# Buffers of TensorE's operands at other addresses, the first weight panel on SyncE's queue, four weight splits at other places

## The chip, the cores and the metric

The program runs on one core of one Trainium2 chip. The metric is the device time of one execution in microseconds (us); a kernel's time is the median of several executions. TensorE (PE) multiplies, VectorE (DVE) and ScalarE (ACT) work on elements, GpSimd (POOL) builds a few tables, and SyncE (SP) issues most DMAs.

## What is computed

Three transformer layers over 256 tokens of width 1024, all in float32. Cut to what matters:

```python
def first_block(x, ...):
    h = x
    for layer in range(2):
        y = rmsnorm(h, norm_g[layer, 0])
        y = gmlp_mixer(y, ...) if layer == 0 else diff_attention(y, ...)
        h = h + rmsnorm(y, norm_g[layer, 1])
        y = rmsnorm(h, norm_g[layer, 2])
        y = conv_ffn(y, ...)                 # D_FF = 2816: (gelu(g) * u) @ w_down
        h = h + rmsnorm(y, norm_g[layer, 3])
    return h

def second_block(x, ...):                    # one layer
    x = x + 0.5 * swiglu(rms_norm(x, ffn1_norm), ...)
    u = rms_norm(x, mix_norm) @ w_in
    a_out = mla_attention(...)               # 8 heads, low-rank q and kv, rope
    b_out = moba_attention(...)              # 8 heads of 64, linear distance bias
    x = x + concatenate([a_out, b_out]) @ w_out
    x = x + 0.5 * swiglu(rms_norm(x, ffn2_norm), ...)
    return rms_norm(x, final_norm)
```

`reference` is `second_block(first_block(x))`. The weights fill 352 panels of 128 x 1024 numbers, 512 KB each, and each is used once.

## The kernel before, in words

**Stages.** The panels run in the order gMLP mixer (`GMLP`, 24), convolutional FFN (`FFN0`, 66), differential attention (`DIFF`, 32), FFN (`FFN1`), SwiGLU FFN (`FFN2`), the MLA and MoBA mixer (`MIX`, 32), SwiGLU FFN (`FFN3`). Between two stages stands a `boundary`: the residual is added, the row is normed and turned by TensorE, and the next stage's first four panels are taken.

**A panel's way.** SyncE's `load(n)` (L312 to L317) brings panel n into one of five `raw` buffers; from the sixth on it first waits until the low split of panel n-5 is done (semaphore `lo`). ScalarE's `upto(last)` (L441) casts each panel up to `last` into `w_high`, in float32r (L448); VectorE's `upto(last)` (L864) subtracts that from `raw` into `w_low` (L868). Both have nine buffers (`RING`). TensorE multiplies `high * x_high + high * x_low + low * x_high`, in float32r. Activations are split in the same way into `x_parts` (X2), `a_high`, `a_low`, `c4_high`, `c4_low`. In every float32r product one operand is a panel and the other an activation part. In the rows, `G<-x_parts,w_high` has `x_parts` moving and `w_high` stationary; `G<-w_high,x_parts` has it the other way round.

**An FFN.** Gate and up panels are multiplied with `wide_tile` (L1407 for the high part against both activation parts, 512 columns; L1411 for the low part, 256 columns). Down panels are multiplied in `rows` (L1487, 512 columns each). The last seven down panels stand at the end of each FFN (`_ffn_order`), and `tail` multiplies them token half by token half.

**Order.** Every engine runs a list that is written out by hand, and semaphores join the lists. Where a split stands in the list of ScalarE or VectorE is set by the calls of `upto` between other steps. A step behind a split waits for it, and a split behind a step waits for the step.

**The start.** TensorE runs itself up with products of `ones` (`run_up(12)`, then `run_up(4)` after the first activation part). ScalarE's queue issues the DMA of panel 0 (L635) and then that of `g0`, the first norm's gains (L636). SyncE issues the turned input `xT` in four parts (L331), panels 1, 2, 3, 4, the relative-position rows, panels 5 and 6, the input and the constants, panel 7, and so on. ScalarE then makes the high activation parts (`x0_high`, L643) and casts the panels; VectorE makes the low ones (`x0_low`, L1075). The first products are L1422 and L1426, the further ones of the first eight panels L1442, L1443 and L1448. Panels 0 to 3 are used for both token halves, then 4 to 7 for the first half, then 4 to 7 for the second.

**The second mixer.** Its heads 8 to 11 (two MoBA heads each) and 12 to 15 (two MLA heads each) run through: scores (L1598, L1599), `combine` (VectorE), `exps` (ScalarE, L614, L616), `turn` (TensorE, L1615), `turned_out` (ScalarE, L627), `weigh_values` (TensorE, L1627 to L1629), `outs` (VectorE, L1314), `pair_out` (TensorE, L1848), `cast` (ScalarE, L811), `low_out` (VectorE, L1322). `pair_out(15)`, the last, waits for `outs(15)` and for `low_out(14)`. `qk_out(10)` (L632, L633) makes what `scores(10)` reads. `B` in the code is `MIX`, so `upto(B + 35)` splits the last of the four panels with which `FFN3` begins. In `boundary(6)` TensorE needs panel B + 35 last of the four.

**Addresses.** The tensors lie one behind the other in the order of their `sb(...)` calls, each start rounded up to 32 bytes. `raw`, `w_high` and `w_low` start at multiples of 64 bytes. `h` follows with 2 x 1026 numbers, 8208 bytes, and so `x_parts`, `a_high`, `a_low`, `c4_high`, `c4_low`, the gains, `big1` and `big2` start 32 bytes beside a multiple of 64. `big2` has 8208 bytes too, after which `big3`, `w3`, `qk` and the tables are at multiples of 64 again. The identity for the turns lies in `cst`, 32 bytes beside.

## Time and profile before

| | us |
|---|---|
| median of 3 runs | 1078.57 |
| lowest, highest | 1077.62, 1079.41 |
| the profiled execution, its own time | 1076.99 |
| its span, first to last instruction | 1075.1 |

The profile is of one execution; the rows' times are counted from its first instruction. 1.9 us of the execution's time lie outside the span. Its granted TensorE clock was 0.999 on the mean. In a row of the timeline stand the start, the time until the last of the row's instructions ended, the engine, the line, the operation, and in brackets how long the engine had been idle and what ended that.

### The profile page before, as it was taken

What the parts mean: (1) busy time and instruction counts of PE and PEld (TensorE: products, weight loads), DVE (VectorE), ACT (ScalarE), POOL (GpSimd) and SP (SyncE); (2) the same over time, 40 slices, a digit from 0 to 9 for tenths busy, and PEclk for the clock granted to TensorE, in tenths of its full rate; (3) what the DMA queues carried; (4) which work ended last, traced back from release to release, by engine and by line L of the source; (5) the groups of instructions that cost most, each with busy time, mean ns of one, the idle gap of its engine ahead of it and who ended that gap; (6) DMA issues with size and microseconds to landing.
All of it is one profiled execution on the core that took longest, in us unless ns stands there. A gap on an engine that the chain in (4) does not pass through costs nothing.

```text
span 1075.1 us, 15630 instructions
## 1 busy us (share of the span) xinstructions
PE 1064.2 (99%) x5976; PEld 910.3 (85%) x5976; DVE 774.0 (72%) x1213; ACT 653.2 (61%) x1176; POOL 36.3 (3%) x39
## 2 busy tenths in 40 slices
PE   8999999999999999999999999999999999999997
PEld 7988888888799878888888888888899878888886
DVE  4898987878767889878787666656676857655663
ACT  5767755666657777666567554445456647444552
POOL 0840000000000000000000000000000000000000
PEclk9999999999999999999999999999999999999999
DMA  9764866655463357656553756665355516656641
GB/s 344 260 199 149 241 203 200 222 181 177 172 219 114 104 159 247 199 179 212 180 197 130 238 176 188 212 197 187 129 171 152 197 58 206 189 192 196 198 157 40
DMA packets 56777, 198.13 MB, mean 184 GB/s; under 512 B 6576, under 2 KB 8536, under 8 KB 56704
## 3 DMA queue, kind: packets, MB, share of 16 engines
q1 hardware_dynamic: 56016, 195.89, 56.3%
q10 hardware_dynamic: 576, 1.05, 0.3%
q8 instruction: 48, 0.79, 0.3%
q14 instruction: 25, 0.20, 0.1%
q0 software_dynamic: 112, 0.20, 0.1%
HBM read 195.35 MB, written 1.25 MB: 183 GB/s over the span
## 4 chain that ended last, share of the span: by engine, by line
PE 95%; ACT 2%; DVE 2%; DMA 1%; issue 0%; ACTq 0%
PE G L1407 28%; PE Y L1487 27%; PE G L1411 14%; PE G L1392 3%; PE G L1394 3%; PE G L1393 3%; PE G L1442 2%; PE G L1448 2%; PE G L1443 2%; PE Y L1482 2%; PE Y L1392 1%; PE Y L1393 1%; PE Y L1394 1%; PE G L1461 1%; PE G L1615 1%; PE Y L1495 1%
## 5 line engine op out<-in xcount | busy, mean ns | idle before, releaser
L868 DVE TENSOR_TENSOR w_low<-raw,w_high 128x1024 fp32r<-128x1024 f32 x352 | 424.5, 1224 | 38.0 <-ACT w_high L448 36.4
L448 ACT CAST w_high<-raw 128x1024 fp32r<-128x1024 f32 x352 | 363.1, 1045 | 13.8 <-DMA raw<-in_panels 8.9
L1407 PE MATMUL G<-x_parts,w_high 128*128 128x512 f32 x1280 | 325.3, 396 | 0.0
L1407 PEld LDWEIGHTS G<-x_parts,w_high 128*128 128x128 f32 x1280 | 233.1, 188 | 49.3
L537 ACT COPY big<-G 128x512 f32<-128x512 f32 x80 | 46.8, 585 | 233.0 <-PE G L1411 233.0
L1411 PEld LDWEIGHTS G<-x_parts,w_low 128*128 128x128 f32 x1280 | 172.7, 188 | 14.6
L1411 PE MATMUL G<-x_parts,w_low 128*128 128x256 f32 x1280 | 175.8, 280 | 0.0
L962 DVE TENSOR_TENSOR w<-G,big 128x512 f32<-128x512 f32 x80 | 55.3, 691 | 161.9 <-ACT big L537 161.8
L1487 PE MATMUL Y<-w_high,a_high 128*128 128x512 f32 x420 | 134.0, 400 | 0.0
L1487 PE MATMUL Y<-w_high,a_low 128*128 128x512 f32 x420 | 132.3, 396 | 0.0
L1487 PE MATMUL Y<-w_low,a_high 128*128 128x512 f32 x420 | 132.1, 395 | 0.0
L1487 PEld LDWEIGHTS Y<-w_high,a_low 128*128 128x128 f32 x420 | 79.0, 188 | 19.1
L1487 PEld LDWEIGHTS Y<-w_low,a_high 128*128 128x128 f32 x420 | 79.0, 188 | 19.1
L1487 PEld LDWEIGHTS Y<-w_high,a_high 128*128 128x128 f32 x420 | 73.0, 188 | 11.4
L989 DVE SCALAR_TENSOR_TENSOR w<-w,par 128x255 f32<-128x255 f32 (+1 forms) x160 | 70.2, 480 | 1.3
L1392 PE MATMUL G<-x_parts,w_high 128*128 128x256 f32 x224 | 63.7, 285 | 0.0
L1393 PE MATMUL G<-x_parts,w_high 128*128 128x256 f32 x224 | 62.6, 280 | 0.0
L1394 PE MATMUL G<-x_parts,w_low 128*128 128x256 f32 x224 | 62.6, 279 | 0.0
L1442 PE MATMUL G<-w_high,x_parts 128*128 128x512 f32 x120 | 48.7, 406 | 0.1
L565 ACT ACTIVATE w<-w,par 128x256 f32<-128x256 f32 x80 | 43.6, 594 | 8.4 <-DVE w L962 8.4
L1443 PE MATMUL G<-w_low,x_parts 128*128 128x512 f32 x120 | 47.5, 395 | 0.0
L1448 PE MATMUL G<-w_high,x_parts 128*128 128x512 f32 x120 | 47.5, 395 | 0.0
(256 smaller groups left out, 1204.8 us busy)
## 6 DMA issues: line engine op xcount, KB each, us to landing
raw<-in_panels SPq DMA_DIRECT2D x351, 512.0 KB, 4.3
gain_pre<-in_gains SPq DMA_DIRECT2D x7, 512.0 KB, 5.8
gain_post<-in_gains SPq DMA_DIRECT2D x4, 512.0 KB, 6.6
big<-in_xT SPq DMA_DIRECT2D x4, 256.0 KB, 7.1
h<-in_x SPq DMA_DIRECT2D x2, 512.0 KB, 7.2
big<-rel_rows SPq DMA_DIRECT2D x8, 128.0 KB, 5.2
raw<-in_panels ACTq DMA_DIRECT2D x1, 512.0 KB, 5.3
big<-in_w_s SPq DMA_DIRECT2D x1, 512.0 KB, 9.3
```

The source lines that it names most:

```text
L448: s.copy(WH[:, n % RING, :], raw[:, n % RAWS, :]).then_inc(hi, 1)
L868: v.tensor_tensor(WL[:, n % RING, :], raw[:, n % RAWS, :], WH[:, n % RING, :].bitcast(F32), ALU.subtract).then_inc(lo, 1)
L989: last = v.scalar_tensor_tensor(out=wb[:, f % 2, m, T - n:T], in0=gate_of(f, m)[:, 0:n], scalar=par[:, c:c + 1], in1=wb[:, f % 2, m, T - n ...
L1392: mm(out, WH[:, j, c:c + w], xh, start=first, stop=False, skip_group_check=skip)
L1393: mm(out, WH[:, j, c:c + w], xl, start=False, stop=False, skip_group_check=skip)
L1394: return mm(out, WL[:, j, c:c + w], xh, start=False, stop=last, skip_group_check=skip)
L1407: mm(out, WH[:, n % RING, k * P:(k + 1) * P], X2[:, k, :, :], start=k == 0, stop=False, skip_group_check=True)
L1411: last = mm(out[:, 0:T], WL[:, n % RING, k * P:(k + 1) * P], X2[:, k, 0, :], start=False, stop=k == KT - 1, skip_group_check=True)
L1442: mm(out, xh, hic, start=k == 0, stop=False)
L1443: mm(out, xh, loc, start=False, stop=False)
L1448: last = mm(out, xl, hic, start=False, stop=k == KT - 1)
L1487: end = mm(Y[:, 2 * t + c, :], x, w[:, j, half(c)], start=start, stop=stop)
```

## The change

1. `x_parts`, `a_high`, `a_low`, `c4_high` and `c4_low` are allocated straight behind `w_low` and ahead of `h`; `h` has rows of 1040 numbers in place of 1026 (still 1025 used), and `big2` 2080 numbers in place of 2052. So all of these, and the tensors up to `par`, start at multiples of 64 bytes. `cst` keeps its 32 bytes beside one.
2. Panel 0's DMA leaves ScalarE's queue and is issued by SyncE, between the first part of `xT` and panel 1. `g0` is now ScalarE's first DMA.
3. In the second mixer the split of panel B + 19 moves on ScalarE from ahead of `exps(9)` to between the two `turned_out` of head 9, and on VectorE from ahead of `outs(8)` to the next call of `upto`, behind `low_out(8)`.
4. At its end, ScalarE casts panel B + 35 behind `cast(15)` and a table load, in place of ahead of `cast(14)`. VectorE splits panel B + 34 behind `low_out(15)` in place of ahead of `outs(14)`, and panel B + 35 in `boundary(6)`, behind its second residual sum, in place of ahead of `outs(15)`.

The ring of nine, the five raw buffers and the seven down panels at an FFN's end are in both kernels.

```diff
         WL = sb("w_low", [P, RING, W], F32R)
-
-        h = sb("h", [P, TT, D + 2])
         X2 = sb("x_parts", [P, KT, 2, T], F32R)
         AH = sb("a_high", [P, KT, T], F32R)
         AL = sb("a_low", [P, KT, T], F32R)
         c4h = sb("c4_high", [P, T], F32R)
         c4l = sb("c4_low", [P, T], F32R)
+
+        h = sb("h", [P, TT, D + 16])
...
-        big2 = sb("big2", [P, 2052])
+        big2 = sb("big2", [P, 2048 + 32])
...
-        sqj = big2[:].rearrange("p (t d) -> p t d", t=TT)
+        sqj = big2[:, 0:TT * (D + 2)].rearrange("p (t d) -> p t d", t=TT)
...
             x_part(0)
-            load(1)
+            load(0), load(1)
...
-            act.dma_start(raw[:, 0, :], io["panels"][0]).then_inc(ld[0], 16)
             act.dma_start(g0[:], io["gain_first"]).then_inc(g0_in, 16)
...
-            upto(B + 19)
+            upto(B + 18)
             exps(9)
             qk_out(10)
-            turned_out(9, 0), turned_out(9, 1)
+            turned_out(9, 0)
+            upto(B + 19)
+            turned_out(9, 1)
             cast(8)
...
                 turned_out(a, 0), turned_out(a, 1)
-                upto(B + 20 + a)
+                if a < 15:
+                    upto(B + 20 + a)
...
             combine(9)
-            upto(B + 19)
+            upto(B + 18)
             outs(8)
...
-                upto(B + 20 + a)
+                if a < 14:
+                    upto(B + 20 + a)
                 outs(a)
```

ScalarE's list at the program's start, before (L643 is `x0_high`, `g` are the first norm's gains):

```order
L635 DMA raw<-in_panels 128x1024
L636 DMA g<-in_gain_first 128x8
L455 ACT_TABLE_LOAD
L455 ACTIVATE junk<-eps 128x1
L643 ACTIVATE x_parts<-big,g 128x256 x2
```

The same place in the changed kernel, where line numbers here are one lower:

```order
L635 DMA g<-in_gain_first 128x8
L455 ACT_TABLE_LOAD
L455 ACTIVATE junk<-eps 128x1
L642 ACTIVATE x_parts<-big,g 128x256 x2
L448 CAST w_high<-raw 128x1024 x2
```

The gains' DMA has become the first, and panel 0's is gone from this queue to SyncE's second place.

ScalarE's list around head 9 of the second mixer, before (L614 and L616 are `exps(9)`, L632 and L633 `qk_out(10)`, L627 `turned_out`):

```order
L448 CAST w_high<-raw 128x1024 x2
L614 ACTIVATE w,sm<-w,nm 128x128
L616 ACTIVATE w,sm<-w,nm 128x256
...
L632 ACTIVATE qk<-G 128x256
L633 COPY qk<-G 128x256
L627 COPY w<-G 128x384 x2
L811 CAST a_high<-Y 128x256
```

The same place in the changed kernel:

```order
L448 CAST w_high<-raw 128x1024
L614 ACTIVATE w,sm<-w,nm 128x128
L616 ACTIVATE w,sm<-w,nm 128x256
...
L632 ACTIVATE qk<-G 128x256
L633 COPY qk<-G 128x256
L627 COPY w<-G 128x384
L448 CAST w_high<-raw 128x1024
L627 COPY w<-G 128x384
L810 CAST a_high<-Y 128x256
```

One of two casts has moved from ahead of the exponentials to between the two copies.

VectorE's list at the end of the second mixer, before (L1314 is `outs`, L1322 `low_out`, L893 the residual sum in `boundary(6)`, L898 and L903 the norm):

```order
L868 TENSOR_TENSOR w_low<-raw,w_high 128x1024
L1314 TENSOR_SCALAR otk<-G,rs 128x64 x4
L1322 TENSOR_TENSOR a_low<-G,a_high 128x256 x2
L893 SCALAR_TENSOR_TENSOR h<-Y,h 128x512 x2
...
L893 SCALAR_TENSOR_TENSOR h<-Y,h 128x512 x2
L898 RECIPROCAL rs<-sd 128x1
```

The same place in the changed kernel, where VectorE's lines are two higher:

```order
L1316 TENSOR_SCALAR otk<-G,rs 128x64 x4
L1324 TENSOR_TENSOR a_low<-G,a_high 128x256 x2
L870 TENSOR_TENSOR w_low<-raw,w_high 128x1024
L895 SCALAR_TENSOR_TENSOR h<-Y,h 128x512 x2
...
L895 SCALAR_TENSOR_TENSOR h<-Y,h 128x512 x2
L870 TENSOR_TENSOR w_low<-raw,w_high 128x1024
L900 RECIPROCAL rs<-sd 128x1
```

No split stands ahead of `outs(15)` any more; one stands behind the two `low_out`, and one behind the second residual sum.

## Rows read from the trace of the kernel before

**Rows 1.** The page: busy time of an engine, then groups with count and mean:

```profile
PE 1064.2 (99%) x5976; PEld 910.3 (85%) x5976; DVE 774.0 (72%) x1213; ACT 653.2 (61%) x1176; POOL 36.3 (3%) x39
L1407 PE MATMUL G<-x_parts,w_high 128*128 128x512 f32 x1280 | 325.3, 396 | 0.0
L1407 PEld LDWEIGHTS G<-x_parts,w_high 128*128 128x128 f32 x1280 | 233.1, 188 | 49.3
L1487 PE MATMUL Y<-w_low,a_high 128*128 128x512 f32 x420 | 132.1, 395 | 0.0
L1487 PEld LDWEIGHTS Y<-w_low,a_high 128*128 128x128 f32 x420 | 79.0, 188 | 19.1
```

**Rows 2.** Timeline of an FFN's stretch, TensorE:

```profile
201.73 2.03 PE L1407 MATMUL G<-x_parts,w_high 128*128 128x512 f32 x8
...
203.60 1.10 PE L1411 MATMUL G<-x_parts,w_low 128*128 128x256 f32 x8
```

**Rows 3.** Timeline of the program's start:

```profile
0.74 0.41 ACTq L635 DMA_DIRECT2D raw<-in_panels  x1
...
1.06 5.49 PE L1639 MATMUL Y<-ones 128*128 128x128 f32 x24 [1.06 <-POOL eps L388]
...
1.18 0.45 ACTq L636 DMA_DIRECT2D g<-in_gain_first  x1
...
7.61 0.91 ACT L643 ACTIVATE x_parts<-big,g 128x256 fp32r<-128x256 f32 x2 [4.45 <-DMA g<-in_gain_first]
...
9.50 2.12 PE L1422 MATMUL G<-w_high,x_parts 128*128 128x512 f32 x8 [0.17 <-ACT w_high L448]
```

**Rows 4.** DMAs issued in the first 1.5 us: size, us from issue to landing:

```profile
raw<-in_panels ACTq DMA_DIRECT2D x1, 512.0 KB, 5.3
...
big<-in_xT SPq DMA_DIRECT2D x1, 256.0 KB, 4.9
g<-in_gain_first ACTq DMA_DIRECT2D x1, 4.0 KB, 6.4
```

**Rows 5.** DMA engines over the first 30 us, 40 equal slices of 0.75 us:

```profile
DMA  0067989999999999898998999999999999999999
```

**Rows 6.** Timeline around panel 7 in the first mixer:

```profile
22.49 1.05 ACT L448 CAST w_high<-raw 128x1024 fp32r<-128x1024 f32 x1 [3.61 <-DMA raw<-in_panels]
...
23.57 1.23 DVE L868 TENSOR_TENSOR w_low<-raw,w_high 128x1024 fp32r<-128x1024 f32 x1 [0.16 <-ACT w_high L448]
...
25.94 0.40 PE L1442 MATMUL G<-w_high,x_parts 128*128 128x512 f32 x1
```

**Rows 7.** Timeline around head 9 of the second mixer:

```profile
808.55 2.00 ACT L448 CAST w_high<-raw 128x1024 fp32r<-128x1024 f32 x2
...
812.07 0.50 PE L1615 MATMUL G<-cst,w 128*128 128x128 f32 x3
812.89 0.50 PE L1598 MATMUL Y<-qk 64*128 64x128 f32 x4 [0.32 <-ACT qk L633]
```

**Rows 8.** Timeline at the second mixer's end, up to `pair_out(15)`:

```profile
870.04 0.39 PE L1629 MATMUL G<-big,w 128*128 128x64 f32 x2
...
870.23 1.23 DVE L868 TENSOR_TENSOR w_low<-raw,w_high 128x1024 fp32r<-128x1024 f32 x1 [3.43 <-ACT w_high L448]
...
871.25 0.63 PE L1487 MATMUL Y<-w_low,a_high 128*128 128x512 f32 x2
871.37 0.85 DVE L1314 TENSOR_SCALAR otk<-G,rs 128x64 f32<-128x64 f32 x4
872.14 0.41 DVE L1322 TENSOR_TENSOR a_low<-G,a_high 128x256 fp32r<-128x256 f32 x1
872.70 0.41 PE L1848 MATMUL G<-cst,otk 128*128 128x128 f32 x2 [0.82 <-DVE a_low L1322]
```

**Rows 9.** Timeline of `boundary(6)`, behind that:

```profile
875.24 1.39 DVE L893 SCALAR_TENSOR_TENSOR h<-Y,h 128x512 f32<-128x512 f32 x2 [1.26 <-PE Y L1482]
...
886.05 0.16 DVE L898 RECIPROCAL rs<-sd 128x1 f32<-128x1 f32 x1 [1.14 <-ACT sd L479]
```

## The prediction

> **What bounds the kernel now.** I read the page first: TensorE is busy for 1064.2 of 1075.1 us [rows 1], so nothing but its own pace, or one of the few places where it waits, can move the time. Its pace next: the weight loads (PEld) run beside the products, and a stretch of an FFN [rows 2] shows eight products of 512 columns from 201.73 to 203.60, 1.87 / 8 = 0.234 us each, with no gap to the next group. Third, where TensorE waits. There are three places worth naming. At the start the first real product comes at 9.50 [rows 3]. In the second mixer `scores(10)` waits for `qk_out(10)` at 812.89 [rows 7], and `pair_out(15)` for `low_out(14)` at 872.70 [rows 8]. The change touches each of the three, and beside them the addresses on which TensorE's pace might depend.
>
> **The addresses.** The case for a gain is that every float32r product has one operand 32 bytes beside a multiple of 64. The rows let me compare the sides. L1407 moves `x_parts`, which is beside, and holds `w_high`, which is not; L1487 moves a panel, which is not, and holds `a_high` or `a_low`, which are. Both products have 512 columns: 396 ns and 395 ns, and both weight loads 188 ns [rows 1]. So a moving operand beside the multiple costs 1 ns at most against one on it, and a stationary one nothing. What these rows can't exclude is that either flaw costs the same, since no float32r product before has both operands at a multiple of 64. That needs two different mechanisms of one size, and I take 0 for this term. The ends of its range are rivals below.
>
> **The start.** ScalarE's first part of `x` begins at 7.61, released by the gains' DMA, which is queued behind panel 0 on ScalarE's queue [rows 3]. It takes 6.4 us from issue to landing for 4 KB, where panel 0 takes 5.3 for 512 KB [rows 4]: panel 0 is there at 0.74 + 5.3 = 6.0, the gains at 7.6. The first part of `xT` is there at 0.74 + 4.9 = 5.6. With the gains first on their queue they are issued at 0.74 and no longer stand behind 512 KB. They can't land later than with panel 0 ahead, and I take them to be there by 5.6, when the `xT` part is. Panel 0 is then second in SyncE's queue, issued at 1.18. The two together are 768 KB, and both queues had carried these 768 KB by 6.0 beside a part of panel 1. I take 6.0 for it. It can't be before `xT`, 5.6. The upper end is 8.3: 5.3 us from the new issue, 6.5, and 256 KB ahead of it at 768 KB in 5.3 us, 1.8 more.
>
> The chain is then: `x` part 5.6 to 6.5 (0.91, as in the row), cast of panel 0 from 6.5, and TensorE 1.0 behind that, 7.5. Before, it was 7.61 + 0.91 = 8.5 and TensorE at 9.50, the same 1.0 behind. The run-up with `ones` ends at about the same time: its first 24 products end at 1.06 + 5.49 = 6.55, and eight more at 0.23 us each, the pace of those, would end at 8.4, at twice that pace, with the clock up, at 7.5. TensorE thus begins 2.0 earlier, or 1.1 in the worst case of the run-up. Of the moved DMA the cost on SyncE is one issue, 0.45 us by the like row on ScalarE's queue, by which its later DMAs slip; they wait in a full queue anyway.
>
> That start isn't kept whole. From the sixth slice of 0.75 us on, the DMA engines are busy for eight tenths or more to the end of the first 30 us [rows 5], so panels land by bytes and not by when TensorE began. Panel 7 is cast at 22.49, after 3.61 us of waiting for its landing, its low split runs from 23.57 to 24.80, and TensorE takes it first at 25.94 [rows 6]: a margin of 25.94 - 24.80 = 1.14. If TensorE comes 2.0 earlier it is there at 23.94 and waits 0.9 us for the split. Of the 2.0 us there remain 1.1. Whether panel 7 lands a little earlier is open: nothing is fetched more, but the ramp of the DMA engines may be better with one big transfer after the other than with two in turn. I take 1.2, with 0.2 (panel 0 and all behind it 1 us later) and 2.0 (panel 7 in time) as ends. Later parts of this mixer aren't pressed: I see no wait of TensorE there.
>
> On which queue a DMA stands the Trainium skill has a rule, in "DMA: Bandwidth & Descriptors", section "Issuing engines are not separate DMA queues": all DMAs run on the same 16 engines and interleave, and several issuing engines save only sequencer time. By that rule the move costs only SyncE's issue, and the bytes ahead of panel 7 stay what they are. The trace agrees so far that panel 0 and the `xT` part, issued at once from two engines, both took some 5 us.
>
> **Head 9.** Two casts of 2.00 us together start at 808.55 on ScalarE, ahead of `exps(9)` and `qk_out(10)`, and TensorE is through with the turn's three products before 812.4 (812.07 plus three at some 0.11) and starts the scores at 812.89 [rows 7]. One cast of 1.0 us goes behind. The exponentials can come up to 1.0 earlier; they also need the row maxima, so I count on at least the 0.5 us that are needed. Gain 0.45, ends 0.3 and 0.5. The cast that moved now stands ahead of `turned_out(9, 1)`. TensorE reads that copy only after two products with panels, over 5 us later. VectorE's split of B + 19 comes later too, and the loads behind it; this panel is used behind the queries of the next heads, more than 10 us on. Cost nothing.
>
> **The mixer's end.** TensorE's last product ahead of the wait starts within the row at 871.25 (two of 0.234), so `pair_out(15)` could begin at 871.72 and begins at 872.70: 0.98 us are lost [rows 8]. The chain: VectorE's split of B + 35 waits 3.43 us for ScalarE's cast and runs 870.23 to 871.46; `outs(15)` stands behind it, to 872.22, and then `low_out(14)`, to 872.55; TensorE follows 0.15 later. Without the split `outs(15)` can begin when the last product of L1629 ends, 870.04 + 0.39 = 870.43, 0.94 earlier than at 871.37. So `low_out(14)` ends at 871.61, and TensorE begins at 871.76 where 871.72 was possible. `cast(14)` on ScalarE isn't late, since its own cast of B + 35 stood ahead and has gone too. Gain 0.94, ends 0.7 and 0.98.
>
> What covers the moved splits. B + 34 goes to the gap ahead of the residual sum: VectorE waits 1.26 us there, just before 875.24 [rows 9], and a split is 1.23. B + 35 goes to behind the second sum, where VectorE waits 1.14 us for ScalarE, at 886.05. It can thus be late by 0.1, which TensorE doesn't see as long as the turns aren't waiting. If a cover is gone, 1.2 us each is the most it costs. Loads of panels B + 39 and B + 40 are issued later, by up to 14 us; they are needed behind five and more panels of 512 KB, at some 3 us each. No cost, 0.5 as the end.
>
> **The sum**, against the profiled execution: 1.2 + 0.45 + 0.94 = 2.6 us from 1076.99, so 1074.4. That execution is 1.6 under the median of the runs, 1078.57, and the forecast is for a median: 1078.57 - 2.6 = 1076.0.
>
> **Rivals.**
>
> *Both operands at 64 bytes make the products faster.* 512 columns at the upper clock, 2.4 GHz, are 213 ns; the rows show 234. If the surplus of 21 ns hung on the one operand that was always beside, it would go. The share is 21 / 234 = 9% of TensorE's 1064 us, 95 us, less what the casts then hold back: about 990. For it: the surplus is real. Against it: it is the same whichever operand is beside [rows 1]. Chance 4%.
>
> For that pace the Trainium skill has a figure, "TensorE: Matmul & The Clock Gate", section "Wait — 56ns, not 53.3ns?": 512 columns are 215.7 ns apart at the full clock. By that the surplus here is 18 ns, and the time would be estimated at some 995. The row's 234 disagrees with the page before any change.
>
> *The reads collide.* With both operands at the same phase, the moving read and the weight load beside it could meet more often. The largest difference between like groups is 1 ns in 395 [rows 1]; for such a collision I double it to 2 ns in 395, 0.5% of 1064 us: 5 us slower, less 2.6, so 1081. It decides from 1 ns per product on. Chance 4%.
>
> *The start gives nothing.* Panel 0 behind `xT` in a slow ramp lands at 7.0 or later, and panel 7 about 1 us later than before: its split ends at 25.8, where TensorE was at 25.94 before. However early TensorE begins, 0.2 us remain. With the mixer's 1.4: 1077.0. For it speaks that the ramp is slow, 5 us for the first transfers. Chance 20%.
>
> *Panel 7 is no hurdle.* One queue ramps better, and the full 2.0 us stay: 1078.57 - 3.4 = 1075.2. Chance 12%.
>
> **How the numbers follow.** The forecast itself has 60%. A difference from no change can be told from 0.2%, 2.2 us, on. The forecast's 2.6 us lies close to this, and the medians scatter by about 0.5, so I give it 45 of its 60 as faster and 15 as same; the fourth rival is faster, the third is same, the first faster and the second slower. Faster 45 + 11 + 4 = 60, same 15 + 1 + 20 = 36, slower 4. For the range, the sum of lower ends is 0.2 + 0.3 + 0.7 - 0.5 = 0.7, of the upper ones 2.0 + 0.5 + 1.0 = 3.5, and a median of before and one of after scatter by 0.5 to 0.9: 1074.2 to 1078.3. The two address rivals, 8%, stay outside.
>
> **What would show it.** Right: the first L1422 at 7.5 instead of 9.50, released by the cast; the gains' DMA no longer in front of L643; a wait of about 0.9 us at panel 7's first product for L868 (L870 there); no wait at L1598 near 812 and none at L1848 near 871; L1407's eight products again in 1.87 us and weight loads of 188 ns. Wrong: eight products in 1.7 us, or 1.9 and more; L1422 after 8.5; panel 7 landing after 23; a new wait of TensorE in `boundary(6)`, at the turns or at B + 35.

## The result: 1065.98 us, and the profile of the changed kernel

| kernel | runs | median, us | range, us | profiled execution, us | its span, us |
|---|---|---|---|---|---|
| before | 4 | 1078.09 | 1077.14 to 1079.41 | 1076.99 | 1075.1 |
| changed | 4 | 1065.98 | 1065.92 to 1066.04 | 1065.92 | 1064.1 |

The ratio is 0.9887, with a 95% interval of 0.987 to 0.9904. The kernel is faster by 12.1 us, where 2.6 were forecast and 1074.2 was the lower end of the range. The part of the forecast on the first panel and the two mixer edits came true; the term that I had set to 0, the addresses, is worth 8 to 9 us.

First the page of the changed kernel, in the groups that answer to [rows 1]. A matmul's line number is 3 higher than before, VectorE's is 2 higher, and L642 was L643. Columns: busy us, mean ns of one, idle us ahead.

```profile
PE 1054.9 (99%) x5976; PEld 914.8 (86%) x5976; DVE 772.8 (73%) x1213; ACT 654.5 (62%) x1176; POOL 35.4 (3%) x39
L1410 PE MATMUL G<-x_parts,w_high 128*128 128x512 f32 x1280 | 319.7, 392 | 0.0
L1410 PEld LDWEIGHTS G<-x_parts,w_high 128*128 128x128 f32 x1280 | 233.9, 188 | 44.4
L1414 PE MATMUL G<-x_parts,w_low 128*128 128x256 f32 x1280 | 178.5, 282 | 0.0
L1490 PE MATMUL Y<-w_low,a_high 128*128 128x512 f32 x420 | 129.7, 390 | 0.0
```

The FFN's product went from 396 to 392 ns and the output product from 395 to 390. These means hold the time of a product from its start to its modelled end, of which a part lies beside the next one. What the program pays is the time from one start to the next. It is read from the timeline of TensorE (start, length, line, operation, count of products in the row), here a stretch of an FFN:

```profile
602.09 0.62 PE L1490 MATMUL Y<-w_high,a_low 128*128 128x512 f32 x2
602.54 0.62 PE L1490 MATMUL Y<-w_low,a_high 128*128 128x512 f32 x2
...
604.36 1.98 PE L1410 MATMUL G<-x_parts,w_high 128*128 128x512 f32 x8
606.18 1.12 PE L1414 MATMUL G<-x_parts,w_low 128*128 128x256 f32 x8
607.13 1.09 PE L1410 MATMUL G<-x_parts,w_high 128*128 128x512 f32 x4
```

Eight products of 512 columns take 606.18 - 604.36 = 1.82 us, where they took 1.87 [rows 2]. The two at 602.09 take 0.45, or 0.225 each. The eight of 256 columns go the other way: 607.13 - 606.18 = 0.95 us, against 0.94 for the same eight in the kernel before:

```profile
604.06 1.11 PE L1411 MATMUL G<-x_parts,w_low 128*128 128x256 f32 x8
605.00 2.03 PE L1407 MATMUL G<-x_parts,w_high 128*128 128x512 f32 x8
```

From the start times of all products, put beside each other one by one in the two traces, the 512-column ones gave 14.5 us (3071 pairs), the 256-column ones took 5.6 (2330), and the rest gave 2.2. I call the mean time from a product's start to the next one's start, over the products of one kind that don't wait and are followed by one of their kind, its **pace**. In these terms 512 columns went from 233.4 ns to between 227.6 and 229.5, and the 256-column products that hold `w_low` (L1411, now L1414) from 117 to 119.

Now the places that the change was made for. The timeline of the start (answers to [rows 3]); the brackets tell how long the engine was idle and what ended that:

```profile
0.74 0.40 ACTq L635 DMA_DIRECT2D g<-in_gain_first  x1
...
1.18 0.89 SPq L317 DMA_DIRECT2D raw<-in_panels  x2
...
5.08 0.91 ACT L642 ACTIVATE x_parts<-big,g 128x256 fp32r<-128x256 f32 x2 [2.41 <-DMA g<-in_gain_first]
...
7.23 2.12 PE L1425 MATMUL G<-w_high,x_parts 128*128 128x512 f32 x8 [0.43 <-ACT w_high L448]
```

The gains are there at 5.08 instead of 7.6, and the first real product comes at 7.23, released by the cast (7.5 forecast, 9.50 before). Around panel 7 (answers to [rows 6]):

```profile
21.57 1.05 ACT L448 CAST w_high<-raw 128x1024 fp32r<-128x1024 f32 x1 [3.62 <-DMA raw<-in_panels]
...
22.65 1.22 DVE L870 TENSOR_TENSOR w_low<-raw,w_high 128x1024 fp32r<-128x1024 f32 x1 [1.79 <-ACT w_high L448]
...
23.06 0.39 PE L1451 MATMUL G<-w_high,x_parts 128*128 128x512 f32 x1
...
23.93 0.50 PE L1445 MATMUL G<-w_high,x_parts 128*128 128x512 f32 x1 [0.48 <-DVE w_low L870]
```

TensorE waits here for the low split, as forecast. The bracket counts from the modelled end of the product ahead; from start to start it is 23.93 - 23.06 = 0.87 us where the pace is 0.23, so 0.64 us are lost and not 0.9. The panel landed 0.9 us earlier than before (its cast starts at 21.57 instead of 22.49). Head 9 (answers to [rows 7]) and the mixer's end (answers to [rows 8]):

```profile
804.52 0.50 PE L1618 MATMUL G<-cst,w 128*128 128x128 f32 x3
804.95 0.50 PE L1601 MATMUL Y<-qk 64*128 64x128 f32 x4
```

```profile
862.86 0.86 DVE L1316 TENSOR_SCALAR otk<-G,rs 128x64 f32<-128x64 f32 x4 [3.66 <-PE G L1632]
...
863.64 0.41 DVE L1324 TENSOR_TENSOR a_low<-G,a_high 128x256 fp32r<-128x256 f32 x1
863.65 0.62 PE L1490 MATMUL Y<-w_low,a_high 128*128 128x512 f32 x2
864.20 0.41 PE L1851 MATMUL G<-cst,otk 128*128 128x128 f32 x2
```

Neither row of TensorE has a bracket any more: the scores follow the turn, and `pair_out(15)` follows the two output products. VectorE's row at 862.86 isn't held by a split but by the product L1632. The list of what TensorE waits for in the whole program (us in total, times, longest) is now this. L1598's 0.3, L1848's 0.8 and the run-up's 1.6 for the first activation part have gone from it, and the two rows of L1498 stood there before, as L1495:

```profile
PE Y L1642 <- POOL eps L388: 1.1, 1, 1.1
PE G L1445 <- DVE w_low L870: 0.7, 2, 0.5
PE G L1425 <- ACT w_high L448: 0.4, 1, 0.4
PE Y L1498 <- DVE w L905: 0.4, 2, 0.2
PE G L1498 <- DVE w L905: 0.2, 1, 0.2
```

### The profile page after: what moved, and what is told of

Read it like the earlier page. It is cut to its first block, busy times and chain, and to the rows that moved or that the text cites. A ratio compares the mean times of both kernels' runs of the same rounds, so it can differ in the third digit from the quotient of the medians.

```text
span 1064.1 us, 15630 instructions
## 1 busy us (share of the span) xinstructions
PE 1054.9 (99%) x5976; PEld 914.8 (86%) x5976; DVE 772.8 (73%) x1213; ACT 654.5 (62%) x1176; POOL 35.4 (3%) x39
## 4 chain that ended last, share of the span: by engine, by line
PE 95%; DVE 2%; DMA 2%; ACT 1%; SPq 0%; issue 0%; ACTq 0%
PE G L1410 28%; PE Y L1490 27%; PE G L1414 14%; PE G L1395 3%; PE G L1396 3%; PE G L1397 3%; PE G L1445 2%; PE G L1446 2%; PE G L1451 2%; PE Y L1485 2%; DMA raw<-in_panels 2%; PE Y L1396 1%; PE Y L1395 1%; PE Y L1397 1%; PE G L1618 1%; PE Y L1498 1%
## 5 line engine op out<-in xcount | busy, mean ns | idle before, releaser
L1410 PE MATMUL G<-x_parts,w_high 128*128 128x512 f32 x1280 | 319.7, 392 | 0.0
L1410 PEld LDWEIGHTS G<-x_parts,w_high 128*128 128x128 f32 x1280 | 233.9, 188 | 44.4
L1414 PEld LDWEIGHTS G<-x_parts,w_low 128*128 128x128 f32 x1280 | 174.6, 190 | 12.5
L1414 PE MATMUL G<-x_parts,w_low 128*128 128x256 f32 x1280 | 178.5, 282 | 0.0
L1490 PE MATMUL Y<-w_high,a_low 128*128 128x512 f32 x420 | 130.0, 390 | 0.0
L1490 PE MATMUL Y<-w_low,a_high 128*128 128x512 f32 x420 | 129.7, 390 | 0.0
L1397 PE MATMUL G<-x_parts,w_low 128*128 128x256 f32 x224 | 63.3, 283 | 0.0
```

What stands on the lines that cost most here:

```text
L1397: return mm(out, WL[:, j, c:c + w], xh, start=False, stop=last, skip_group_check=skip)
L1410: mm(out, WH[:, n % RING, k * P:(k + 1) * P], X2[:, k, :, :], start=k == 0, stop=False, skip_group_check=True)
L1414: last = mm(out[:, 0:T], WL[:, n % RING, k * P:(k + 1) * P], X2[:, k, 0, :], start=False, stop=k == KT - 1, skip_group_check=True)
L1490: end = mm(Y[:, 2 * t + c, :], x, w[:, j, half(c)], start=start, stop=stop)
```

## The experiments

The first question is which part of the change the 12.1 us belong to. The second, which took most of the runs, is what it is about the addresses. Three theories stand:

- **Multiple of 64.** An operand at a multiple of 64 bytes is read faster.
- **Distance.** What counts is where the moving operand lies against the stationary one, counted modulo some number of bytes. Absolute addresses don't count.
- **Other buffers.** The gain comes from `h`, the gains or `big`, which moved too, and reach TensorE through VectorE and ScalarE.

### The change in two halves

`addresses_only` is the kernel before with the new places of the buffers and nothing else:

```diff
-        h = sb("h", [P, TT, D + 2])
         X2 = sb("x_parts", [P, KT, 2, T], F32R)
...
+        h = sb("h", [P, TT, D + 16])
         gP = sb("gain_post", [P, D])
...
-        big2 = sb("big2", [P, 2052])
+        big2 = sb("big2", [P, 2048 + 32])
```

> The kernel before with the first point of the change alone (the addresses). Theory A, the addresses set the pace of the float32r products: in the changed kernel the products of 512 columns came closer together and those of 256 columns a little further apart, -14.5 and +5.6 us between the two traces; so 1078.1 - 9 = 1069, with eight products of L1407 in about 1.8 us in place of 1.87 and the 256-column ones 0.120 us apart in place of 0.117. Theory B, the lists and the start did it in some way that the pace only reflects: 1078 and the pace of before.

Measured: 1069.77 us beside 1077.79 for the kernel before on the same chip, ratio 0.9926 (0.9911 to 0.9941). The pace is that of the changed kernel (512 columns 392 ns on the page, 256 columns 282):

```profile
L1407 PE MATMUL G<-x_parts,w_high 128*128 128x512 f32 x1280 | 319.7, 392 | 0.0
L1411 PE MATMUL G<-x_parts,w_low 128*128 128x256 f32 x1280 | 178.5, 282 | 0.0
```

So the addresses alone give 8.0 us between the medians. `lists_only` is the reverse, the changed kernel with the old places:

```diff
+        h = sb("h", [P, TT, D + 2])
         X2 = sb("x_parts", [P, KT, 2, T], F32R)
...
-        h = sb("h", [P, TT, D + 16])
...
-        big2 = sb("big2", [P, 2048 + 32])
+        big2 = sb("big2", [P, 2052])
```

> The kernel before with the other three points alone (panel 0 on SyncE's queue, the moved splits), addresses as before. By the prediction's own sum 1078.1 - 2.6 to 3.1 = 1075 to 1075.5; the first real product at 7.2, no wait near the end of the second mixer; the pace of before, 0.234 and 0.117 us. Theory B: 1066 to 1068.

Measured: 1074.93 us, ratio 0.9971 (0.9959 to 0.9982), 2.9 us less than before, with the pace of before (396 and 280 ns on the page). The first panel and the two edits are thus worth what was forecast, 2.6.

The halves give 8.0 + 2.9 = 10.9 where the whole gives 12.1. A part of the rest is at the start of `addresses_only`. The timeline of its TensorE, and windows of 2 us (columns: length, busy time of PE with the count, PEclk, DMA share, GB/s):

```profile
7.98 1.16 PE L1639 MATMUL Y<-ones 128*128 128x128 f32 x8 [1.69 <-ACT x_parts L643]
9.32 3.66 PE L1422 MATMUL G<-w_high,x_parts 128*128 128x512 f32 x8 [0.17 <-ACT w_high L448]
```

```profile
8.00:10.00 2.00, 1.82 (x10) 0.83 1.02 411
10.00:12.00 2.00, 2.00 (x6) 0.50 1.03 411
12.00:14.00 2.00, 2.00 (x9) 0.82 0.98 353
```

The granted clock falls to 0.50, which is the lower level of 1.2 GHz, behind an idle time of 1.69 us in the run-up. The trace of the kernel before has the same idle time at 1.62 us and kept 1.00 in these windows. The eight products need 12.82 - 9.32 = 3.50 us where they need 11.47 - 9.50 = 1.97 in the trace of before, so 1.5 us are lost here. The changed kernel has no idle time in its run-up, and its clock is 1.00 in the windows from 6 to 14 us.

The sum is best drawn from the spans of the profiled executions, where it is seen who lost this time. The addresses give 1075.1 - 1067.8 = 7.3, and 7.3 + 1.5 = 8.8 without the loss; the lists give 2.3; and 8.8 + 2.3 = 11.1 stands against 1075.1 - 1064.1 = 11.0 for the whole. The medians say 12.1, probably because other executions of the kernel before pay at the start, too: of the seven beside `x192_a0_timed`, four have a mean granted clock of 0.997 and spans of 1075.9 to 1076.1, and three have 0.998 or 0.999 and 1074.9 to 1075.1. That fits a loss of 1 us in the four, though no trace of such an execution was kept. So the medians' 8.0 isn't to be raised by the whole 1.5.

### Which buffers, and whether a multiple of 64 counts

In all further kernels the changed kernel is the base, and unused buffers between the others move them. A gap of n elements moves all that lies behind it by 4n bytes. Panels means `w_high` and `w_low`; x means `x_parts`; a means `a_high` and `a_low`. But for `x192_a0_timed` each was executed once, and the executions of one kernel lie up to 2.3 us apart (those of the changed kernel 0.12). The readings below therefore rest on the paces in the traces, and the times are beside them. The paces come again: the profiled executions of `x192_a0` and `x192_a0_timed`, the same kernel, agree to 0.1 ns in the FFN's products.

`parts_at_32` puts x and a back to 32 bytes beside, and leaves `h`, the gains and `big` at multiples of 64:

```diff
+        sb("gap_x", [P, 8])
         X2 = sb("x_parts", [P, KT, 2, T], F32R)
...
+        sb("gap_h", [P, 8])
         h = sb("h", [P, TT, D + 16])
```

> The changed kernel with 32 bytes more ahead of x_parts and again ahead of h: x_parts, a_high, a_low, c4 start 32 bytes beside a multiple of 64, panels, h, the big buffers and all else at multiples. Theory A1, it is the operands of the float32r products alone: about 1075, the pace of before. Theory A2, it is the other buffers' addresses (h, the gains, big1, big2, which ScalarE and VectorE use): 1066 and the new pace.

Measured: 1075.07 us, with the pace of before (its page: L1412, which is L1410 moved by two lines):

```profile
L1412 PE MATMUL G<-x_parts,w_high 128*128 128x512 f32 x1280 | 325.3, 396 | 0.0
```

That is `lists_only` within 0.14 us. The other buffers' places don't matter, and the third theory falls. `all_at_32` puts the panels beside too, so that no operand of a float32r product lies at a multiple of 64:

```diff
+        sb("gap_w", [P, 8])
         WH = sb("w_high", [P, RING, W], F32R)
...
+        sb("gap_h", [P, 8])
         h = sb("h", [P, TT, D + 16])
```

> The changed kernel with 32 bytes more ahead of w_high and again ahead of h: panels' splits and activation parts all start 32 bytes beside a multiple of 64. Theory of the multiple: each operand has to be at a multiple of 64, so as slow as before or slower, 1075 or more. Theory of the phase: only the distance between moving and stationary operand matters, modulo 64, and it is 0 here as in the changed kernel: 1066.

Measured: 1066.06 us, against 1065.98 with everything at 64:

```profile
L1412 PE MATMUL G<-x_parts,w_high 128*128 128x512 f32 x1280 | 319.7, 392 | 0.0
L1416 PE MATMUL G<-x_parts,w_low 128*128 128x256 f32 x1280 | 178.5, 282 | 0.0
```

The multiple of 64 falls as an explanation. All operands 32 bytes beside it are as fast as all of them on it. What these two runs have in common with the changed kernel, and `parts_at_32` has not, is that panels and parts lie alike.

### Modulo what: the theory that fell

The distance could count modulo 64 bytes. Four runs asked for that. `x_at_32` moves x alone by 32 and leaves a at a multiple of 64:

```diff
+        sb("gap_x", [P, 8])
         X2 = sb("x_parts", [P, KT, 2, T], F32R)
+        sb("gap_a", [P, 8])
         AH = sb("a_high", [P, KT, T], F32R)
```

> The changed kernel with x_parts alone 32 bytes beside a multiple of 64, and a_high and a_low at multiples. Theory of the phase (the distance of moving and stationary operand, modulo 64): the products with x_parts go back to 0.2333 us per 512 columns and 0.117 per 256, those with a_high and a_low keep 0.227 to 0.229. From the classes' sums: x_parts 512 columns +5 +1 +2.6 us, 256 columns -4.5, so about 1066 + 4.5 = 1070. If one address decided for all classes, 1066 or 1075.

Measured: 1074.25 us. The products with x fell back, as expected. But those with a, which is at a multiple of 64 like the panels, fell back as well, to 233 ns from 228.5. In this kernel a lies 64 bytes further than the panels when both are counted modulo 256. `parts_at_64` puts x there, too:

```diff
+        sb("gap_x", [P, 16])
         X2 = sb("x_parts", [P, KT, 2, T], F32R)
...
+        sb("gap_h", [P, 16])
         h = sb("h", [P, TT, D + 16])
```

> The changed kernel with x_parts, a_high, a_low, c4 64 bytes on: still at multiples of 64, but no longer of 128 as the panels. Theory of the phase modulo 64: 1066, the new pace. Phase modulo 128 or more: another pace, 1070 and more.

Measured: 1068.85 us. Two kernels whose operands all lie at multiples of 64, and 2.9 us between them: modulo 64 falls. The page shows that the kinds of products have come apart:

```profile
L1412 PE MATMUL G<-x_parts,w_high 128*128 128x512 f32 x1280 | 321.0, 393 | 0.0
L1416 PE MATMUL G<-x_parts,w_low 128*128 128x256 f32 x1280 | 174.2, 278 | 0.0
L1492 PE MATMUL Y<-w_low,a_high 128*128 128x512 f32 x420 | 131.9, 395 | 0.0
```

The product that moves x is at 393 ns, near the changed kernel's 392, and the one that holds a is at the 395 of before. The 256-column one is at 278 ns, better than in either kernel. `parts_at_16` cuts a slice out of larger buffers, `a_low` like `a_high`:

```diff
-        X2 = sb("x_parts", [P, KT, 2, T], F32R)
-        AH = sb("a_high", [P, KT, T], F32R)
+        X2 = sb("x_parts", [P, KT * 2 * T + 16], F32R)[:, 4:4 + KT * 2 * T].rearrange("p (k l t) -> p k l t", k=KT, l=2)
+        AH = sb("a_high", [P, KT * T + 16], F32R)[:, 4:4 + KT * T].rearrange("p (k t) -> p k t", k=KT)
...
```

> The changed kernel with x_parts, a_high and a_low read from 16 bytes behind a multiple of 64 on. Phase theory with a pace that goes in steps between 0 (0.2267 and 0.120 us) and 32 (0.2333 and 0.117): something between, 1066 to 1075. Theory that only one multiple counts: 1075 or slower. A faster one is possible too if 0 isn't the best phase.

Measured: 1068.63 us. Since each of these buffers grew by 64 bytes, x lies at 16, `a_high` at 80 and `a_low` at 144, which I had not seen ahead of the run. `low_panels_at_32` puts only `w_low` beside a multiple of 64. It moves by 32 bytes, and all that lies behind it by 64:

```diff
+        sb("gap_l", [P, 8])
         WL = sb("w_low", [P, RING, W], F32R)
+        sb("gap_x", [P, 8])
         X2 = sb("x_parts", [P, KT, 2, T], F32R)
```

> The changed kernel with w_low alone at 32: the low products of an FFN's gate and up (L1414, 256 columns, w_low stationary) should go back from 0.120 to 0.117 us, 1280 of them, -3.5 us; those with w_low moving (L1490 and L1446, 512 columns, 576 of them) from 0.227 to 0.2333, +3.5; the third of the 256-column products with w_low stationary -1. So 1065 to 1066.5. If the read that collides is that of the next product's weights, the ends shift by a product, and the sums don't.

Measured: 1071.47 us, a miss by 5 us. Its x and a lie 64 bytes beyond `w_high` and 32 beyond `w_low`, so no product of it has distance 0.

### A scan of the distance

Distance is written from here on as **s**, the address of the moving operand less that of the stationary one. In an FFN x moves and a panel is held, so s is what x lies beyond the panels. In the output products, and in those for q and k, the panel moves, and s is the negative of what a or x lies beyond. The next eight kernels differ in two gaps only. The first of them:

```diff
+        sb("gap_x", [P, 16])
         X2 = sb("x_parts", [P, KT, 2, T], F32R)
+        sb("gap_a", [P, 112])
         AH = sb("a_high", [P, KT, T], F32R)
```

> The changed kernel with a gap of 64 bytes ahead of x_parts and 448 ahead of a_high: x_parts now lies 64 bytes off the panels' buffers when both are counted modulo 512, the activations' parts lie at the panels' own residue. Theory at this point: the pace of a product hangs on the distance between its two operands, and not on a multiple of 32 or 64 bytes, since x at 32 with a at 64 gave 233 ns in both classes. It expects the a products at 227 to 229 ns as after the change, the FFN's products with x_parts moving at 229.6 and the 256-column ones at 116.2 to 117.6 as with both at 64, the q and k products with x_parts stationary at 233: about 1062.5. Rival (the pace is set by a whole stretch of products whatever their own buffers are): 1066 to 1069.

Measured: 1065.56 us. The a products went to 228 to 229, as expected, and q and k to 233.2. The x products came out slower than in `parts_at_64`, with both buffers at the same places as there (230.4 against 229.6 ns for 512 columns, 117.5 against 116.2 for 256). So the place isn't all; I come back to this. The time is 3 us above the 1062.5 expected and nearer to the rival's 1066. The x products, 1271 of 512 columns and 1922 of 256, account for it: 1271 x 0.8 + 1922 x 1.3 ns = 3.5 us.

```diff
+        sb("gap_x", [P, 32])
         X2 = sb("x_parts", [P, KT, 2, T], F32R)
+        sb("gap_a", [P, 32])
         AH = sb("a_high", [P, KT, T], F32R)
```

> x_parts 128 bytes and the activations' parts 256 bytes off the panels' residue, modulo 512. Theory A (what counts is the distance modulo 128): both classes as after the change, 226.7 to 229 ns for 512 columns and 119 to 120 for 256: 1066.0. Theory B (modulo 256): the a products stay at 227 to 229, the x products go to 233 and 117: about 1068. Theory C (only modulo 512, or an own value for each distance): both at 230 to 234: 1069 to 1075.

Measured: 1069.86 us; the a products at 226.9 to 228.7, the x products at 232.5, which is what modulo 256 asks for in each kind, though the sum is 1.9 us above the 1068 that I had worked out for it, since 256 columns stayed at 118.6 where I had set 117.

```diff
+        sb("gap_x", [P, 64])
         X2 = sb("x_parts", [P, KT, 2, T], F32R)
+        sb("gap_a", [P, 32])
         AH = sb("a_high", [P, KT, T], F32R)
```

> x_parts 256 bytes and the activations' parts 384 bytes off the panels' residue, modulo 512. Theory A (distance modulo 128): 1066.0 with 227 to 229 ns in both classes. Theory B (modulo 256): x products at 227 to 229 and 119 to 120, a products at 233: 1071. Theory C (modulo 512 or an own value for each distance): 1069 to 1075.

Measured: 1069.70 us; x products at 229.2 and 119.1, exactly the changed kernel's, a products at 230.7 to 232.6. Modulo 256 again.

```diff
+        sb("gap_x", [P, 112])
         X2 = sb("x_parts", [P, KT, 2, T], F32R)
+        sb("gap_a", [P, 8])
         AH = sb("a_high", [P, KT, T], F32R)
```

> x_parts 448 bytes (64 short of the panels' residue) and the activations' parts 480 bytes (32 short) off, modulo 512. If the distance counts without its sign, the x products go as with both at 64 (229.6 in the FFN, 256 columns at 116.2 to 117.6) and the a products as at 32 (233.3): about 1070. If the sign counts, so that moving x above the panels is another case than moving it below, the q and k products (x_parts stationary) and the FFN's (x_parts moving) change places: q and k at 229 to 230, the FFN's at 233: 1069 to 1074.

Measured: 1068.69 us. The case in which the sign counts came true: q and k 229.3 to 229.8, where the FFN's are 232.7. And something that nobody asked for: 256 columns at 114.4 ns. With a back at distance 0 the two gains should add:

```diff
+        sb("gap_x", [P, 112])
         X2 = sb("x_parts", [P, KT, 2, T], F32R)
+        sb("gap_a", [P, 16])
         AH = sb("a_high", [P, KT, T], F32R)
```

> x_parts 64 bytes below the panels' residue modulo 512, the activations' parts at it. If each class of products follows its own two operands: the FFN's 512-column products at 232.7 ns and its 256-column ones at 114.4 as in x448_a480, q and k at 229.8, the output products at 227 to 229.5 as after the change; from the counts, 1271 x 3.6 ns + 400 x 1.8 ns - 1922 x 4.8 ns - 158 x 2.9 ns = -4.4 us against 1066.0: about 1061.6. If instead one class sets the pace of the others (the whole stretch), the output products are above 231: 1066 to 1069.

Measured: 1061.77 us, where 1061.6 was worked out from the paces. The next three kernels differ from this diff only in the two numbers: 48 and 80, 120 and 8, 96 and 32.

> x_parts at +192, which is 64 below the panels' residue counted modulo 256. Theory (operands' distance counts modulo 256, as +256 gave the same as 0): the same paces as with +448, 232.7 / 114.4 / 229.8 ns, about 1061.6. Rival (modulo 512): a value of its own, 256 columns at 116 to 119: 1065 to 1068.

Measured: 1061.22 us, with 232.8 / 114.5 / 229.6 ns. A distance of 192 does what 448 does.

> x_parts 32 bytes below the panels' residue. At 32 above, 512 columns took 232.4 to 233.4 and 256 took 117.1 to 117.4; with the sign counting, q and k (stationary x) take here what the moving x took there, 232.4 to 233.4, and the moving x a value of its own: by the neighbours 0 (229.1, 119.1) and -64 (232.7, 114.4) it lies between, 230 to 233 and 114 to 119: 1062 to 1067.

Measured: 1069.75 us, a miss. q and k took 233.4 as expected, but the moving x took 233.1 and 118.5: the value at -32 doesn't lie between its neighbours where I had put it.

> x_parts at +384, which is 128 modulo 256. Theory (modulo 256): as with +128, 232.5 ns for the FFN's 512 columns, 118.6 for 256, 232.6 for q and k; with the output products at 227 to 229.5 that is 1271 x 3.4 + 400 x 4.5 - 2080 x 0.7 ns = +4.7 us on 1066.0: 1070.7. Rival (modulo 512): other values, 1062 to 1069.

Measured: 1069.90 us (1070.7 worked out), with 232.5 / 118.6 / 232.5 ns, those of 128.

The scan, in ns of pace, worked out from the start times in each trace. It goes by s alone, and takes the kernels in which both panel buffers lie alike. The right column is for the 256-column products that hold `w_low`:

```text
s, bytes, modulo 256    512 columns                              256 columns (x moves)
   0                    227 to 229.5 (x, a, q and k)             119
 +16                    231.6 (x)                                116.3
 -16                    229.9 to 230.7 (q and k)                 -
 +32                    232.4 to 233.4 (x, a, q and k)           117.1 to 117.5
 -32                    233.1 to 233.7 (x, a, q and k)           118.5
 +64                    229.6 to 230.8 (x), 228.3 to 230.2 (q,k) 116.2 to 117.5
 -64                    232.7 (x), 233.0 to 233.5 (a, q and k)   114.4 to 114.6
 -80                    231.3 (a_high)                           -
+112                    232.5 (a_low)                            -
 128                    232.5 (x, q and k), 230.7 to 232.6 (a)   118.6
```

The kernel before has s = +32 where x moves and s = -32 where a or x is held. The changed one has 0 everywhere. At s = +64, 229.6 was measured with x moving, and where a panel moves and x is held, at the same s, 229.6 to 230.0 for `w_high`. That is why I take s, and not the place of any buffer, for what counts in the main. At 128 the a products are up to 2 ns faster than those with x, so s doesn't settle all of it. That a common move of all operands changes nothing was tried once, by 32 bytes at s = 0 (`all_at_32`).

### Timed: the best version

`x192_a0_timed` is `x192_a0`, executed four times.

> The same kernel as x192_a0, timed in five rounds. Theory (distance modulo 256): 1061.2 to 1061.8, a ratio to before of 0.9845 and 0.4% under the change as it was made. Rival (single executions of 1061.2 and 1061.8 were luck): 1065 to 1066.

Measured: 1062.18 us (1061.33 to 1062.59), ratio to before 0.9859 (0.9843 to 0.9876). It is 3.8 us below the changed kernel's 1065.98, measured in another set of runs beside 1078.09 for the kernel before (1077.77 here). The runs of the two don't overlap (1065.92 was the changed kernel's lowest); the intervals of the two ratios overlap by a hair (up to 0.9876 here, from 0.987 there). The same stretch of its timeline:

```profile
602.22 2.03 PE L1412 MATMUL G<-x_parts,w_high 128*128 128x512 f32 x8
604.09 1.08 PE L1416 MATMUL G<-x_parts,w_low 128*128 128x256 f32 x8
605.00 2.02 PE L1412 MATMUL G<-x_parts,w_high 128*128 128x512 f32 x8
```

512 columns are back at 604.09 - 602.22 = 1.87 us for eight, and the 256-column eight take 0.91 where the changed kernel takes 0.95. The output products keep the changed kernel's pace (389 ns on the page):

```profile
L1492 PE MATMUL Y<-w_low,a_high 128*128 128x512 f32 x420 | 129.4, 389 | 0.0
```

### Own operands or also the neighbours'

The last run puts `w_low` alone at another place, so that x moves 64 below `w_low` (the best for 256 columns) and at 0 to `w_high` (the best for 512):

```diff
+        sb("gap_l", [P, 16])
         WL = sb("w_low", [P, RING, W], F32R)
+        sb("gap_x", [P, 48])
         X2 = sb("x_parts", [P, KT, 2, T], F32R)
```

> Only w_low lies 64 bytes above the other operands' residue modulo 256, so x_parts lies 64 below it. Theory own (each product follows its own two operands): the FFN's 256-column products with w_low 114.5 ns as at -64, its 512-column ones 229.1 as after the change, the output products w_low with a_high 229.6 (moving 64 above stationary), the other two 228 to 229: from the counts 1066.0 - 1486 x 4.6 ns + 420 x 2.4 ns + 138 x 1.8 ns = 1060.4. Theory neighbours (the weights of the next product are loaded beside it, so alternating products of a triple disturb one another): the FFN's as above, but the triples at 231 to 233 in all three members: 1064 to 1065.5.

Measured: 1067.20 us, and both theories missed. The 512-column products with `w_high` are at 229.1, as expected. The 256-column ones with `w_low` are at 117.8, not at 114.5, though their own distance is the -64 that gave 114.5 in three other kernels. In the timeline (201.13 to 202.07) eight of them take 0.94 us:

```profile
201.13 1.11 PE L1416 MATMUL G<-x_parts,w_low 128*128 128x256 f32 x8
202.07 0.63 PE L1492 MATMUL Y<-w_high,a_high 128*128 128x512 f32 x2
```

The output triples fell to 229.4 to 233.0, where all three are at 227.6 to 229.5 with every operand at 0; that one is at least partly what the second theory says. `low_panels_at_32`, the other kernel whose panel buffers lie apart, leaves the table as well: its q and k products with `w_low` at s = -32 take 235.0.

The start times of the 256-column eights tell more. In `x192_a0_timed`, of the 160 eights, 155 take 798 to 805 ns for seven steps, and 5 take 824 or 825. In `w_low_at_64`, 156 take 824 or 825 and 4 take 793 or 799. Both kernels know both patterns, and each pattern is regular to a nanosecond behind its first steps (118, 117, 118, 118 ns and so on, or 113, 114, 113). So at one distance, and at the same addresses, there is more than one steady rhythm. In both kernels the rare one stands only behind a 512-column eight that had itself been held up (seven steps of 1709 ns or more, where 1588 to 1634 are usual).

The changed kernel's 512-column eights are of two such kinds as well: 60 of 152 need 1586 or 1587 ns for seven steps, 226.7 each, and 89 need 1614 or 1615. These two are told apart by what ran ahead. All 60 of the first kind follow an output product, as the eight at 604.36 does, and all 89 of the second follow a 256-column eight, as the next one does:

```profile
606.18 1.12 PE L1414 MATMUL G<-x_parts,w_low 128*128 128x256 f32 x8
607.13 2.00 PE L1410 MATMUL G<-x_parts,w_high 128*128 128x512 f32 x8
608.97 1.11 PE L1414 MATMUL G<-x_parts,w_low 128*128 128x256 f32 x8
```

It takes 608.97 - 607.13 = 1.84 us where the one ahead took 1.82. `addresses_only`, `all_at_32` and `x256_a384` show the same split, 60 against 90. So within a kernel the group ahead goes with the rhythm. That it is also why `w_low_at_64` differs from `x192_a0_timed`, whose 512-column products run ahead at s = -64 instead of 0, is my reading: in these two the place of `w_low` against `w_high` and a differs, too, and no run parts the two causes. The same reading would explain `x64_a0` beside `parts_at_64`, where x at the same place ran at two paces: only a had moved, whose products go ahead of many of the FFN's.

What in the chip makes the rhythm I can't show. The obvious picture is that the moving operand's reads and those of the weight load beside them meet, and that they keep or lose step by their distance. It fits that a common move of all operands changed nothing and that 256 bytes more gave the same, but no run took the weight loads away, so this stays a picture and isn't shown.

## Why the prediction was wrong, point by point

**The addresses: the step that failed.** The text compares L1407 and L1487, finds 396 against 395 ns and 188 against 188 [rows 1], and concludes that a moving operand beside the multiple costs "1 ns at most against one on it, and a stationary one nothing". The remaining case, that either flaw costs the same, "needs two different mechanisms of one size, and I take 0 for this term". It needs one mechanism only. Both products have their two operands 32 bytes apart, one at s = +32 and one at s = -32, and the scan gives 233.1 to 233.7 ns for both. Equal numbers on two sides of a comparison said that the two sides share something, and I read them as the absence of a cost. The question that was missing is which quantity has the same value in both groups, and has another value after the change. The distance between the operands is that quantity. In its own terms the step could have been held open, since the text itself says that no product before has both operands alike; a value of 0 with 4% on each side was not what such a gap supports. The term measured 8.0 us between the medians, and 8.8 between the profiled spans without the clock's loss at the start.

**The rival "both operands at 64 bytes make the products faster"** had the sign, and a size of 95 us. It took the whole surplus over 213 ns as the price of the one operand beside. Of the 21 ns, 4 to 6.7 went, in 512 columns only. `all_at_32` shows that its mechanism is not the one either. The Trainium skill's 215.7 ns for 512 columns ("TensorE: Matmul & The Clock Gate", section "Wait — 56ns, not 53.3ns?") is not reached at any distance tried here: the fastest steady pattern of an eight is 226.7.

**The rival "the reads collide"** expected a loss of 2 ns when both operands have the same phase. For 256 columns that happened, 117 to 119 ns and 5.6 us in all. For 512 columns the same change had the other sign, and these have the larger sum.

Beside this stands a rule of the Trainium skill: TensorE has two independent read ports into SBUF, and "Loading the next tile's weights doesn't steal SBUF read bandwidth from the running matmul" ("TensorE: Matmul & The Clock Gate", section "Step-by-step: what each phase is for"). By it no distance between the two operands should matter. The measurement differs: moving the buffers alone (`addresses_only`) took the products of 512 columns from between 232.8 and 233.8 ns to between 227.5 and 229.5, whatever the mechanism is.

**The start: right in its end by luck, with two errors that cancel.** First product 7.23 (7.5 forecast), hurdle at panel 7 as named. But the panel landed 0.9 us earlier, on which the text had kept its options open, and 0.64 us were lost at panel 7 instead of 0.9. In `lists_only`, where the old pace brings TensorE there later, it was 0.4, so that 1.9 us were left behind it and not 1.1. Then came a wait that the text had ruled out ("Later parts of this mixer aren't pressed"). The timeline of `lists_only` at 60 us:

```profile
59.57 0.40 ACT L682 CAST a_high<-big 128x256 fp32r<-128x256 f32 x1 [0.76 <-DVE big L1148]
59.95 0.30 PEld L1490 LDWEIGHTS Y<-w_high,a_high 128*128 128x128 f32 x2 [0.74 <-issue]
59.98 0.70 PE L1490 MATMUL Y<-w_high,a_high 128*128 128x512 f32 x2 [0.57 <-issue]
```

The profile names no releaser here ("issue"), but the first output product starts as ScalarE's cast of `a_high` ends, 59.57 + 0.40 = 59.97. That cast stands behind elementwise work whose time didn't shift with TensorE's. 0.7 us go here, and 1.1 remain of the start, where 1.2 were forecast. In the changed kernel the same place costs 0.24 us: there TensorE begins its last product ahead of it at 59.54 instead of 59.13, by its slower 256-column products.

**Head 9: right.** 0.39 us, 0.45 forecast; the scores follow the turn with no wait.

**The mixer's end: right.** 0.9 us, 0.94 forecast. The two moved splits have their cover: no new wait of TensorE stands in the list, and `boundary(6)` shows none that wasn't there before.

**The sum of these three** was to be 2.6 us. `lists_only` gave 2.3 between the spans of the profiled executions (1075.1 to 1072.8) and 2.9 between the medians.

**The range** reached to 1074.2, since both address rivals stayed outside. The time with the old addresses, 1074.93, lies in it.

## What to carry to other kernels

When two groups in a profile have the same duration though they differ in what is suspected, look for what they share before calling the suspect free of cost, above all where no group shows the state that the change brings about. On this kernel the distance between the moving and the stationary operand, counted modulo 256 bytes, moves a 512-column float32r product between 227 and 234 ns and a 256-column one between 114 and 119. A tuned kernel that is bound by TensorE can be scanned for it with unused buffers of a few bytes at no other cost, kind by kind, and once the pace of each kind at a distance had been measured, the sum over kinds foretold three further runs to 0.2 to 0.8 us. Where it hadn't, or where what ran ahead changed, the sums missed: by 2 us in `x128_a256`, by 3 in `x64_a0`, and by 5 and 7 in the two kernels whose panel buffers lay apart. So a version found this way has to be measured, not summed.

## What was not expected of the hardware

- The pace depends on the distance of the two operands with its sign and with a period of 256 bytes: +64 gives 229.6 to 230.8 ns, -64 gives 232.7 to 233.5 (512 columns), 192 does what 448 does, 256 what 0 does, 384 what 128 does.
- The best distance isn't the same for the two widths: 0 for 512 columns (227 to 229.5), -64 for 256 columns (114.5 against 119 at 0).
- At one distance there are several steady rhythms, 113.5 and 117.7 ns in the case of 256 columns at -64, 226.7 and 230.6 ns in that of 512 columns at 0, and the latter go with the group ahead.
- A DMA of 4 KB took 6.4 us behind 512 KB in its queue [rows 4] and 4.3 us without:

```profile
big<-in_xT SPq DMA_DIRECT2D x1, 256.0 KB, 4.1
g<-in_gain_first ACTq DMA_DIRECT2D x1, 4.0 KB, 4.3
```

- An idle time of 1.69 us in the run-up was followed by a granted clock of 0.50 in one kernel, and one of 1.62 by a clock of 1.00 in another, both in the first 12 us of the program. The changed kernel has no such gap, and its four executions lie within 0.12 us of each other, where those of the kernel before lie within 2.3.
